# Three odd-sized SBUF buffers padded, which moves every buffer behind them

## The reference

```python
for i in range(2):
    h = rmsnorm(x, attn_norm_g[i])
    if i == 0: mix = stick_breaking_attention(h, w_qkv, w_o)       # 2048 -> 6144, 16 heads of 128, 2048 -> 2048
    else:      mix = dsa_attention(h, w_in, ..., w_o)              # indexer, top-64 keys, 4 kv heads, 2048 -> 2048
    x = x + mix
    h = rmsnorm(x, ffn_norm_g[i])
    u = h @ w_up[i]                                                # 2048 -> 11264
    gate, val = split(depthwise_causal_conv3(u))
    x = x + (silu(gate) * val) @ w_down[i]                         # 5632 -> 2048
```

## Time and profile before

| | |
|---|---|
| three runs | 2278.26, 2281.96, 2282.38 us |
| median | 2281.96 us |
| the profiled execution's own time | 2278.08 us |
| its span, first to last instruction | 2276.3 us |
| TensorE matmul busy | 2246.2 us, 99% of the span |
| VectorE busy | 1508.8 us, 66% |
| ScalarE busy | 1169.4 us, 51% |
| mean busy share of the DMA engines on the weight queue | 54% |
| granted TensorE clock, mean | 0.998 |

### The profile page before, as it was taken

How to read it: one execution, slowest core, us unless ns; L and a number is a source line. 1 busy time by engine, 2 the same in 40 slices (tenths; PEclk the granted TensorE clock), 3 DMA queues, 4 the chain that set the end, 5 groups by cost and what they waited for, 6 DMA issues and landing times.

```text
span 2276.3 us, 36358 instructions
## 1 busy us (share of the span) xinstructions
PE 2246.2 (99%) x13240; PEld 1985.5 (87%) x13240; DVE 1508.8 (66%) x1768; ACT 1169.4 (51%) x1401; POOL 2.6 (0%) x9
## 2 busy tenths in 40 slices
PE   7999999999999999999999999999999999999998
PEld 6999998888888888888889888888888888888887
DVE  6565656677777777555567887766777777774443
ACT  6555555555555555444454455555555555553342
POOL 0000000000000000000000000000000000000000
PEclk9999999999999999999999999999999999999999
DMA  6454545555555565555555544455655555556553
GB/s 225 158 166 157 166 160 173 186 180 197 185 190 193 180 197 181 196 191 186 187 196 190 180 151 136 132 201 167 203 178 196 184 191 192 183 195 199 198 196 119
DMA packets 113106, 411.99 MB, mean 181 GB/s; under 512 B 12688, under 2 KB 12816, under 8 KB 113040
## 3 DMA queue, kind: packets, MB, share of 16 engines
q1 hardware_dynamic: 111168, 404.80, 54.0%
q10 hardware_dynamic: 1296, 4.13, 0.5%
q0 software_dynamic: 576, 2.10, 0.3%
HBM read 408.88 MB, written 2.10 MB: 181 GB/s over the span
## 4 chain that ended last, share of the span: by engine, by line
PE 94%; DVE 4%; ACT 1%; issue 1%; DMA 0%; DVEq 0%; ACTq 0%; POOL 0%
PE psum L969 94%; DVE w_lo L567 1%; ACT w_hi L245 1%; DVE gates L579 0%; DVE rb L739 0%; DMA xres<-x_in 0%; DVE xg L575 0%; DVE score L785 0%; DVE rb L753 0%; PE psum L1182 0%; DVE qr L745 0%; DVE tu L731 0%; DVE ra L757 0%; DVE ra L737 0%; DVE tu L729 0%
## 5 line engine op out<-in xcount | busy, mean ns | idle before, releaser
L567 DVE TENSOR_TENSOR w_lo<-raw,w_hi 128x1024 fp32r<-128x1024 f32 x772 | 937.7, 1224 | 704.8 <-ACT w_hi L245 699.0
L969 PE MATMUL psum<-xg,w_hi 128*128 128x512 f32 (+1 forms) x3936 | 1362.9, 392 | 12.1 <-DVE xg L575 12.1
L245 ACT CAST w_hi<-raw 128x1024 fp32r<-128x1024 f32 x772 | 804.6, 1049 | 816.3 <-PE psum L969 815.4
L969 PE MATMUL psum<-xg,w_lo 128*128 128x256 f32 (+1 forms) x3936 | 1095.7, 278 | 0.0
L969 PEld LDWEIGHTS psum<-xg,w_hi 128*128 128x128 f32 x3936 | 738.0, 188 | 166.7 <-DVE xg L575 12.7
L969 PEld LDWEIGHTS psum<-xg,w_lo 128*128 128x128 f32 x3936 | 745.6, 189 | 2.4 <-issue 2.2
L969 PE MATMUL psum<-hid,w_hi 128*128 128x512 f32 x1408 | 493.0, 393 | 0.0
L969 PE MATMUL psum<-hid,w_lo 128*128 128x256 f32 x1408 | 392.9, 279 | 0.0
L969 PEld LDWEIGHTS psum<-hid,w_hi 128*128 128x128 f32 x1408 | 263.8, 187 | 62.9
L969 PEld LDWEIGHTS psum<-hid,w_lo 128*128 128x128 f32 x1408 | 263.8, 187 | 0.0
L969 PE MATMUL psum<-att,w_hi 128*128 128x512 f32 x512 | 180.2, 394 | 0.1
(11 more groups left out here) (135 smaller groups left out, 956.2 us busy)
## 6 DMA issues: line engine op xcount, KB each, us to landing
raw<-w_all SPq DMA_DIRECT2D x772, 512.0 KB, 3.3
xres<-x_in ACTq DMA_DIRECT2D x4, 512.0 KB, 9.5
out_t<-xres POOLq DMA_DIRECT2D x4, 512.0 KB, 3.6
cst<-consts_in ACTq DMA_DIRECT2D x2, 768.0 KB, 10.2
vecs<-vecs_in ACTq DMA_DIRECT2D x1, 354.0 KB, 12.1
avg_d<-consts_in ACTq DMA_DIRECT2D x1, 64.0 KB, 11.8
vecs<-vecs_in ACTq DMA_DIRECT2D x1, 32.0 KB, 4.3
```

The source lines that it names most:

```text
L245: act.copy(w_hi[:, c % RING, :], raw[:, c % RING, :]).then_inc(hi_ready, 1)
L567: dve.tensor_tensor(w_lo[:, c % RING, :], raw[:, c % RING, :], f32(w_hi[:, c % RING, :]), ALU.subtract).then_inc(lo_ready, 1)
L969: return pe.matmul(o, lhsT, rhs, start=start, stop=True, skip_group_check=True)
```

## The change

`vecs` grows from 772 to 1104 elements, `rs` from 258 to 272, and a row of `upad` from 258 to 264. Every use of them names the old extent, so no instruction is added, removed or given another shape; only `upad`'s row step is 24 bytes longer.

```diff
-        vecs = sb("vecs", [P, NV + 1])
+        vecs = sb("vecs", [P, 1104])
         avg_d = sb("avg_d", [P, P])
-        rs = sb("rs", [P, T + 2])
+        rs = sb("rs", [P, 272])
         part = sb("part", [P, 4, T])
-        upad = sb("upad", [P, 4, T + 2])
+        upad = sb("upad", [P, 4, 264])
...
-                act.activation(rs[:, :], psum[:, bank, 0:T + 2], ACT.Sqrt, bias=eps_ap).then_inc(root_ready, 1)
+                act.activation(rs[:, 0:T + 2], psum[:, bank, 0:T + 2], ACT.Sqrt, bias=eps_ap).then_inc(root_ready, 1)
...
-            act.dma_start(vecs[:, V_CONV:], vecs_in[:, V_CONV:]).then_inc(vecs_in_s, 16)
+            act.dma_start(vecs[:, V_CONV:NV + 1], vecs_in[:, V_CONV:]).then_inc(vecs_in_s, 16)
...
-                dve.reciprocal(rs[:, :], rs[:, :]).then_inc(rs_ready, 1)
+                dve.reciprocal(rs[:, 0:T + 2], rs[:, 0:T + 2]).then_inc(rs_ready, 1)
```

## The result

The changed kernel takes 2292.01 us (median of ten runs, 2287.68 to 2307.93) against 2278.05 us of the one before (now ten runs, 2275.96 to 2282.38, the three shown above among them): ratio 1.0062, 95% interval 1.0046 to 1.0078. It is slower, where 0.28% faster was forecast, and outside the stated 2271.8 to 2282.2. Its ten times lie at three levels: 2287.7 (three), 2291.7 to 2292.8 (five) and 2307.5 to 2307.9 (two). The profiled execution took 2287.68 us, 9.6 us more than the 2278.08 of the one before.

A forecast was written before the change was run, and what follows sets the result against it. TensorE's matmul beat was taken as the bound; 4.69 (down-projections) + 0.80 - 0.05 + 0.85 (output projections) + 0.16 (settling) = 6.45 us off the 2281.96 median gave 2275.5 us, range 2271.8 to 2282.2.

The forecast's parts named there:

- The bound: Whole kernel: TensorE's matmuls busy 99% of the span; in two long stretches time is pairs of matmuls times the beat.
- The beats: TensorE's pairs take 346.7 ns over `xg`, 350.0 over `att` and `hid`, 3.3 apart, ascribed to where the rows start.
- The rival "no effect": The beat belongs to something other than the start's residue; time stays at 2282.0 us; chance 0.12.
- the doubt that the memory's half makes the 3.3 ns: `att` and `hid` lie in the upper half, `xg` in the lower; if that made the beat, nothing changes.
- blocks of 64 bytes: Access in blocks of 64 bytes or more: a 2048-byte row of `att` or `hid` touches 33 blocks instead of 32.
- should simply go on in `xg`'s beat: Both down-projections, entered straight from the up-projections: 1408 pairs at 3.33 ns less, 4.69 us gained.
- the first output projection has the same two interruptions in the same places: First output projection: 16 pairs slower (0.05 us lost), 240 quicker behind `l0_tri` and `l0_av` (0.80 us gained).
- I take 0, the beats being the same in each of seven pairs of heads: Layer 0's query and key pieces over `xg`: no change, bounded by 2.24 us lost and 1.17 us gained.
- 2816 pairs of up-projection never go slow: Both up-projections: argument against the slower case, since their `stat` is followed by the quick beat in the old kernel.
- The rival "slower": Slow beat holds through the second layer's long stretch: up-projection +9.39 us, net +9.3 us, 2291.3 us; chance 0.08.
- Second output and down-projection: Second layer's long stretch: about 3.2 us shorter, with the output projection gaining 0.85 us if quick throughout.
- VectorE and ScalarE: Durations of their groups should not change by more than 1 or 2 ns; any gain would hide behind TensorE.

## Why the prediction was wrong

**The bound: right.** In the long stretches the time is the count of pairs times the beat; TensorE is busier by 10.0 us and the kernel takes 9.6 more.

**The beats: right, and the start of the rows decides them.** 350.0 ns belonged to `att`'s and `hid`'s place, and they took on `xg`'s beats as forecast. The rival "no effect" is out; the doubt that the memory's half makes the 3.3 ns was answered by the runs that put `att` and `hid` at 32, where they have 346.7 ns. Its blocks of 64 bytes were not the unit: 640 is a multiple of 64 and has 351.1 ns.

**The down-projections "should simply go on in `xg`'s beat": right, and the trap.** They went on, in the slow beat in the first layer: +2.30 us instead of -2.35.

**The step that failed: "the first output projection has the same two interruptions in the same places", so quick behind `l0_av`, and the beats of the query and key pieces at "I take 0, the beats being the same in each of seven pairs of heads".** Seven equal pairs of heads were seven looks at one layout. The change moves the operands of just those interruptions, from 96 to 0 modulo 256, and behind the new `l0_av` the beat is slow in all seven and in the output projection, 353.3 ns. With it failed "2816 pairs of up-projection never go slow": they had always been entered from `att` at 350.0, and with `gates` and `avg_d` in the old places `stat` turns a slow beat quick. The change took away both. The run with 1440 bytes in front of `att` shows the second; for the first the runs show that `att` at 0 hands on the slow beat and at 350.0 was followed by a quick up-projection four times of four.

**The rival "slower" had the mechanism and the price, in the other layer.** It gave +9.39 us for an up-projection, and the first one took 9.38. It asked for an output projection that ends slow and a `stat` that does not break it, and both came, in the first layer. That its net of 9.3 us is so near the 9.6 of the profiled executions is partly luck: the 1.1 us lost in layer 0's pieces, which it left out, are about what the start and layer 1's keys and queries gave back. I had given it a chance of 0.08, where two beats at one start deserved far more: with two of them and several new interruptions ahead of each long stretch, the forecast was a guess at which. Against it stood that both `stat`s are followed by the quick beat, but in the kernel before they are entered from it too, so this said nothing of what they do to the slow one. The second layer then goes slow too, in some executions, and that was in no case of mine (15.4 us more).

**Small terms.** Second output and down-projection: 3.07 us gained in the stretch, 3.2 forecast; that the second layer was quick in the profiled execution was one of two outcomes. VectorE and ScalarE: unchanged, as forecast. Layer 0's pieces: 1.1 us lost in a stated bound of 2.24.

**What stays open.** Why 256 bytes, and why 32 or 160 hold the quick beat alone; why the place of the small matmuls' operands chooses as the table for layer 0 has it, and what would hold for other matmuls; and what differs between two executions of one program so that the second layer takes the one or the other.

## What to carry to other kernels

When TensorE is the bound, read the spacing of matmul starts by buffer, not the durations: mean durations of 393 ns in the first down-projection and 391 in the first up-projection hid a beat of 350.0 against 346.7. If one buffer has two steady beats, a layout that can fall into either is not a gain even where the better one was seen; look for the distance between activations and weights at which only the better one is held (here 32 bytes modulo 256), with a bare run of a few hundred microseconds, and put all the streamed buffers there. And "rounder" addresses are no aim in themselves. A beat that is the same in many repeats of one layout says nothing of the next layout.

## What was not expected of the hardware

Pairs of matmuls at a multiple of 256 bytes have one of two rhythms, 346.7 or 353.3 ns, also on a core with nothing else at work, and here held one for as long as nothing broke in, over 2072 pairs (732 us) behind the first layer's `stat`. Which of them can differ between two executions of one program, and is worth 16 us here. Rows 4 bytes off the weights' start take 353.3 to 360.0 ns, up to 3.8% above the best; 16 and 24 bytes reach 360.0 too, behind some widths.
